# State space's inputs: seven products for six chunks a layer instead of five, their sums of weights on VectorE instead of GpSimd

## The chip, the cores and the metric

The kernel runs on one core of a Trainium2 chip. The metric is the device time of one execution in microseconds; the median of three runs is given, and one more execution was profiled. The core's engines have their own instruction queues and meet only at semaphores: TensorE (PE; its weight loads are listed as PEld), VectorE (DVE), ScalarE (ACT), GpSimd (POOL) and SyncE (SP), which issues the loads of the weights.

## The reference, cut to what matters

Two models of two layers each work on 256 tokens of width 1024, all in float32. The change touches the first model's two layers, in one place: the multiplication of the normed input by the columns of `w_in` that are the inputs of the state space (`xbc`, 3072 columns), the convolution with four taps after it, and silu.

```python
u = rms_norm(h, mix_norm[l])
(z_s, xbc, dt_s, qkv, z_d, b_d, a_d, gate_s, gate_d) = jnp.split(u @ w_in[l], split_points, axis=-1)
...
xbc = jax.nn.silu(causal_depthwise_conv(xbc, conv_w, conv_b))
xs, Bm, Cm = jnp.split(xbc, [SSM_INNER, SSM_INNER + SSM_GROUPS * SSM_STATE], axis=-1)
...
dt = jax.nn.softplus(dt_raw.astype(f32) + dt_bias.astype(f32))
a = -jnp.exp(a_log.astype(f32))
y = ssd_chunked(xs, dt, a, Bm, Cm) + xs.astype(f32) * d_skip.astype(f32)[:, None]
```

## The kernel before, in words

**Chunks.** All weights come from HBM in chunks of 128 x 2048 floats (sixteen tiles of 128 x 128, 1 MB) into a ring of three slots. SyncE loads chunk c once TensorE has begun chunk c-2 (`stream`). Each chunk gives 256 output features for 256 tokens. The twelve chunks of `xbc` are called steps 0 to 11 here; two layers have them, so whatever happens in one layer happens twice.

**Plain or by seven.** A plain chunk is sixteen products of a 128 x 128 weight tile with 256 tokens (`Tensor.product`). A chunk "by seven" (`Tensor.seven`) sees the chunk as a 2 x 2 matrix of blocks and uses Winograd's form of Strassen's method: seven block products in place of eight, each of four tiles with 128 tokens, 28 in all. For it someone must make, beforehand, four sums of weight blocks (the tile `s` in the arena: `s1` to `s4` here, of which `s1` and `s2` come from the first instruction), and, once per stage, four sums of the tokens (`tokens_by_dve`, four instructions, L1103 to L1108). Afterwards VectorE puts the quarters of the result together from two PSUM banks (`join`, L1122 to L1133, four instructions), after ScalarE has copied one quarter out (`part_by_act`, L1017).

**Who waits for the sums.** In the usual order of the seven products TensorE takes B11, B21 and T4 first (24 of 56 records), waits for the first instruction's sums (`summed(2)`), takes T3, waits for the second's (`summed(3)`), takes T2 and T1, and waits for the last (`summed(4)`). In the first chunk of a stage (`new`) the order is another: B11 and B21 (16 records), then at once the wait for all four sums, then B22, T1, T2, T3, T4.

**The steps.** `BY_SEVEN` lists the steps that go by seven, 2, 5, 6, 9 and 10 before. Steps 0 and 1 are multiplied before the norm is known and scaled by VectorE (`pair_opened_by_dve`, L1032). TensorE then multiplies the 48 small columns (`small`, L1999), goes through steps 2 to 11, with transposes of a finished step beside them (`rows`, L2007), and takes the first chunk of the gate z (`z_s` 0). Then it needs the silu of the last step (`features_ready` 12) for the products `cb` (L2039), and VectorE's copy of the first of these (L1703) before it may fill the same bank with `seg` (L2047).

**VectorE's queue.** In this order: norm (L912), scaling of steps 0 and 1, the tokens' sums, the chain that makes the time steps dt from `small` (L1568 to L1601, handing over to ScalarE four times), and then for each step, if it is by seven, the join, and for every step the convolution: six `scalar_tensor_tensor` (L1621), three taps for two tiles, in place. The convolution waits for ScalarE, which first writes the product with the fourth tap and the bias (L1270 for a joined step; L1278 and L1284 for a plain one, which ScalarE reads from PSUM itself). After each step ScalarE makes silu (L1289). After step 11 VectorE waits for a small exponential of ScalarE (`eg1`, L1340), makes the sums of weights for z's first chunk by seven, and copies `cb` (L1703).

**Sums by GpSimd.** For the five steps by seven of each layer the sums of weights are made by GpSimd (`weights_by_pool`, L1086 to L1090). Everywhere else `weights_by_dve` and `last_weights_by_dve` make them on VectorE (L1070, L1072, L1058). A semaphore of each engine counts its sums; `SUMMED` says how many there were before a chunk.

```python
    for n in range(12):
        if n in BY_SEVEN:
            join(v, m.seven_xbc, L, "xbc_7", BY_SEVEN.index(n), in_place=True)
            if ROWS_AT <= n < ROWS_AT + 8:
                rows(n - ROWS_AT)
        conv(n)
```

Of the kernel before, what the change touches and what calls it, by code (L numbers as in the profile page):

```python
# [12 lines left out]
ALU = mybir.AluOpType  # L13
AX = mybir.AxisListType

P = 128
S = 256
# [3 lines left out]
DEPTH = 2  # L21
# [4 lines left out]
RING = 3  # L26
# [115 lines left out]
GROUPS = 4  # L142


class Sems:


    def __init__(self, ctx, nc):
        self.nc, self.all = nc, []

        def sem(name):
            self.all.append(ctx.enter_context(nc.semaphore(name)))
            return self.all[-1]
# [81 lines left out]
        self.angles_ready = sem("angles_ready")  # L235
        self.rotary_ready = sem("rotary_ready")
        self.sum_by_dve = sem("sum_by_dve")
        self.sum_by_pool = sem("sum_by_pool")
        self.tx_by_dve = sem("tx_by_dve")
        self.th_ready = sem("th_ready")  # L240
        self.pool_step = sem("pool_step")
# [10 lines left out]

BY_SEVEN = (2, 5, 6, 9, 10)
Z_SEVEN = (1, 2, 3, 4, 5, 6, 7)
Q_SEVEN = (1, 2, 4, 5, 7, 8, 10, 11)

# [38 lines left out]
class Tensor:  # L297
# [96 lines left out]
    def seven(self, sums, f, at, X, Y, acts, first, last, ready=None, new=False, by_token=False):  # L394


        e, sems = self.e, self.sems
        if at[0] == 0:
            self.whole = self.chunk()
        a = lambda i, g: self.whole[:, (i * GROUPS + g) * P:(i * GROUPS + g + 1) * P]  # L400
        s = lambda i, g: sums.s[:, f % 2, SUM_OF[i], g * P:(g + 1) * P]
        part = lambda bank, i: bank[:, i * P:(i + 1) * P]

        def product(bank, i, weights, what, fresh, stop):
            for g in at:
                if ready:
                    ready(what, g)

                both = (acts(what, g), weights(g)) if by_token else (weights(g), acts(what, g))
                ins = self.mm(part(bank, i), *both, fresh and g == at[0], stop and g == at[-1])  # L410
            return ins

        def summed(n):
            e.wait_ge(sems.sum_by_pool if f in BY_POOL else sems.sum_by_dve, 4 * SUMMED[f] + n)

        def finished(ins):
            if last:
                ins.then_inc(sems.bulk_done, 1)

        product(X, 0, lambda g: a(0, g), "B11", first, False)  # L420
        product(X, 1, lambda g: a(1, g), "B21", False, False)
        if ready:
            summed(4)
            product(Y, 3, lambda g: s(4, g), "B22", first, False)
            if new:
                product(Y, 1, lambda g: s(1, g), "T1", False, False)
            finished(product(X, 2, lambda g: s(2, g), "T2", False, last))
            product(Y, 2, lambda g: s(3, g), "T3", False, False)
            if not new:
                product(Y, 1, lambda g: s(1, g), "T1", False, False)  # L430
            finished(product(Y, 0, lambda g: a(3, g), "T4", False, last))
        else:
            product(Y, 0, lambda g: a(3, g), "T4", first, False)
            summed(2)
            product(Y, 2, lambda g: s(3, g), "T3", False, False)
            summed(3)
            finished(product(X, 2, lambda g: s(2, g), "T2", False, last))
            product(Y, 1, lambda g: s(1, g), "T1", False, False)
            summed(4)
            finished(product(Y, 3, lambda g: s(4, g), "B22", False, last))  # L440
# [237 lines left out]
def loads(c):  # L678

    return c // RING + (c % RING > 0)  # L680
# [36 lines left out]
    multiply_fast(_L, "down", _at + CHUNKS2 - KF // 2, KF // 2, PAIRS, False)  # L717


BY_POOL = {FAST_FROM[_L, "xbc_7"] + _i for _L in range(DEPTH) for _i in range(len(BY_SEVEN))}  # L720
SUMMED = [sum((_g in BY_POOL) == (_f in BY_POOL) for _g in range(_f)) for _f in range(len(FAST))]


def feed(L, name):
# [336 lines left out]
def weights_by_dve(v, seven, ring, f, last=True):  # L1061
# [10 lines left out]
    e.tensor_tensor(s[:, 2, :], s[:, 1, :], w[:, 0, :], ALU.add).then_inc(sems.sum_by_dve, 1)  # L1072
    if last:
        last_weights_by_dve(v, seven, ring, f)


def weights_by_pool(g, seven, ring, f):

    e, sems, c = g.e, g.sems, FAST[f]
    w = ring[:, c % RING, :].rearrange("p (i n) -> p i n", i=4)  # L1080
    s = seven.s[:, f % 2]
    e.wait_ge(sems.w_loaded[c % RING], 16 * loads(c))
    if f >= 2:

        e.wait_ge(sems.w_used, FAST[f - 2] + 1)
    e.tensor_tensor(s[:, 0:2, :], w[:, 2:3, :].to_broadcast([P, 2, GROUPS * P]), w[:, 0:4:3, :], ALU.add).then_inc(sems.sum_by_pool, 2)  # L1086
    e.wait_ge(sems.sum_by_pool, 4 * SUMMED[f] + 2)
    e.tensor_tensor(s[:, 2, :], s[:, 1, :], w[:, 0, :], ALU.add).then_inc(sems.sum_by_pool, 1)
    e.wait_ge(sems.sum_by_pool, 4 * SUMMED[f] + 3)
    e.tensor_tensor(s[:, 3, :], w[:, 1, :], s[:, 2, :], ALU.add).then_inc(sems.sum_by_pool, 1)  # L1090


def tokens_by_dve(v, m, seven, n, at):

    v.e.wait_ge(v.sems.x_ready, scaled(n) + KD)
    sums_by_dve(v, m.xT, seven, at)
# [431 lines left out]
def first_dve(v, m, m2, L, par, par_next, cst, ring, ones):  # L1528
# [33 lines left out]
    for i in range(2):  # L1562
        pair_opened_by_dve(v, m, L, "xbc", i, m.pad[:, i, :, 3:3 + S])
    tokens_by_dve(v, m, m.seven_xbc, 3 * L + 1, TOKENS_FROM[L, "xbc_7"])
    e.wait_ge(sems.chain_done, CHAIN.filled(L, "small", 0))
    b = bk[CHAIN.bank(L, "small", 0)]
    t = lambda i: m.tmp[:, i]
# [98 lines left out]


    for n in range(12):
        if n in BY_SEVEN:
            join(v, m.seven_xbc, L, "xbc_7", BY_SEVEN.index(n), in_place=True)  # L1670
            if ROWS_AT <= n < ROWS_AT + 8:
                rows(n - ROWS_AT)
        conv(n)
        if ROWS_AT <= n < ROWS_AT + 8 and n not in BY_SEVEN:
            rows(n - ROWS_AT)
        if n == CUM_AT:
            running_sums()
        if n == CUM_T_AT:
            e.wait_ge(sems.chain_done, CHAIN.filled(L, "cum_t", 0))
            b = bk[CHAIN.bank(L, "cum_t", 0)]  # L1680
            e.tensor_copy(m.acT[0:3 * SPREAD, :], b[0:3 * SPREAD, 0:S]).then_inc(sems.chain_read_dve, 1)
# [266 lines left out]
def first_pool(g, m, m2, L, cst, ring):  # L1948

    e, sems, seen = g.e, g.sems, g.seen  # L1950
    feed_by_pool(g, m, L, "ffn1")
    for i in range(len(BY_SEVEN)):
        weights_by_pool(g, m.seven_xbc, ring, FAST_FROM[L, "xbc_7"] + i)
    e.wait_ge(sems.chain_done, CHAIN.filled(L, "kq", 3))
    e.memset(m.inv64[0:BASE, :, BASE:2 * BASE], 0.0)
    e.wait_ge(sems.diag_turned, upto(L, "diag_turned", 1))
    e.tensor_copy(m.inv64[0:BASE, :, 0:BASE], m.diag[0:BASE])
    e.tensor_copy(m.inv64[BASE:2 * BASE, :, BASE:2 * BASE], m.diag[BASE:2 * BASE]).then_inc(sems.diag_ready, 1)
    seen.up("diag_ready")
    if L == DEPTH - 1:  # L1960
        e.wait_ge(sems.mem_squared, KD)
        n = KD // 2
        while n:
            ins = e.tensor_tensor(m2.memx[:, 0:n, :], m2.memx[:, 0:n, :], m2.memx[:, n:2 * n, :], ALU.add)
            n //= 2
            if n:
                ins.then_inc(sems.pool_step, 1)
                e.wait_ge(sems.pool_step, seen.up("pool_step"))
            else:
                ins.then_inc(sems.mem_summed, 1)  # L1970
    feed_by_pool(g, m, L, "ffn2")
    seen.check(L)
# [1201 lines left out]
```

## Time and profile before

| | |
|---|---|
| median of three runs | 3200.02 us (3200.02 to 3201.71) |
| the profiled execution | 3200.47 us, of which the span is 3198.7 us |
| TensorE busy | 3180.1 us, 99% of the span; mean granted clock 0.999 |
| VectorE busy | 2349.5 us, 73% |
| ScalarE busy | 663.8 us, 21% |
| GpSimd busy | 278.7 us, 9% |
| weights loaded | 460 whole chunks of 1 MB, median 4.9 us from issue to landing |

The span counts from the first to the last instruction; 1.8 us of the execution lie around it. "Busy" is the time in which an engine had an instruction under way. Matmuls in float32 stand as two records each. Matmul durations overlap their neighbours, so a group's length is best read as the distance from its start to the next group's start. "[0.28 <-DVE arena L1703]" behind a row means that the engine sat idle for 0.28 us before it and that this instruction ended the wait. "x12" is the number of records that a row merges.

### The profile page before, as it was taken

The page shows a single profiled execution, that of the slowest core. Times are in us where ns is not written, and L with a number is a line of the kernel's source. Part 1 is how long each engine was busy: PE and PEld are TensorE (multiplying, and loading weights), DVE is VectorE, ACT ScalarE, POOL GpSimd, SP SyncE. Part 2 cuts the span into 40 slices and gives each one's busy share as a digit, 9 for nine tenths or more (in the row PEclk, how much of TensorE's full clock was granted, in tenths as well). Part 3 has the DMA queues.
Part 4 walks back from the last instruction along what each step waited for, and adds up shares of the span by engine and source line. Part 5 has one row for each costly group of instructions (what it writes and reads, how often), then busy time and mean ns, then how long its engine had stood idle before and what let it go on. Part 6 is the DMA issues. An engine that isn't in the chain of part 4 may idle for free.

```text
span 3198.7 us, 59387 instructions
## 1 busy us (share of the span) xinstructions
PE 3180.1 (99%) x25152; PEld 3032.9 (95%) x25152; DVE 2349.5 (73%) x4622; ACT 663.8 (21%) x1627; POOL 278.7 (9%) x329
## 2 busy tenths in 40 slices
PE   9999999999999999999999999999999999999998
PEld 9999999899999999998999999889999999889998
DVE  6657887376666578873867898877786988876885
ACT  1113433211111134332211111212211111212211
POOL 0202000001102020000011000300031000300031
PEclk9999999999999999999999999999999999999999
DMA  5544444345444443443544454343444444343443
GB/s 204 172 158 137 141 150 154 110 161 172 170 161 170 159 145 133 160 146 112 184 171 172 159 172 170 120 155 138 158 166 165 169 165 169 123 154 132 159 171 132
DMA packets 89786, 497.51 MB, mean 156 GB/s; under 512 B 25104, under 2 KB 29616, under 8 KB 30640
## 3 DMA queue, kind: packets, MB, share of 16 engines
q1 hardware_dynamic: 70752, 489.45, 44.2%
q10 hardware_dynamic: 18768, 4.25, 0.7%
q8 instruction: 199, 3.26, 0.4%
q14 instruction: 67, 0.55, 0.0%
HBM read 491.55 MB, written 2.11 MB: 154 GB/s over the span
## 4 chain that ended last, share of the span: by engine, by line
PE 89%; DVE 8%; ACT 1%; issue 1%; DMA 1%; ACTq 0%; SPq 0%; DVEq 0%
PE bank L358 82%; DVE arena L1070 2%; DVE arena L1058 1%; DVE arena L1072 1%; ACT arena L2430 1%; DVE arena L2702 1%; DVE arena L1125 1%; PE bank L2068 1%; DVE arena L1131 1%; DVE arena L2709 1%; DVE arena L1122 0%; PE bank L2863 0%; PE bank L2122 0%; PE bank L2807 0%; PE bank L2844 0%
## 5 line engine op out<-in xcount | busy, mean ns | idle before, releaser
L358 PE MATMUL bank<-arena 128*128 128x128 f32 x9384 | 1109.9, 275 | 2.2 <-DVE arena L1058 2.2
L358 PEld LDWEIGHTS bank<-arena 128*128 128x128 f32 x9384 | 1078.1, 192 | 2.9 <-DVE arena L1058 2.9
L358 PE MATMUL bank<-arena,ring 128*128 128x128 f32 (+1 forms) x6360 | 994.8, 309 | 2.0 <-ACT arena L876 1.9
L358 PEld LDWEIGHTS bank<-arena,ring 128*128 128x128 f32 x6360 | 900.0, 191 | 58.3 <-issue 2.9
L358 PE MATMUL bank<-xT,ring 128*128 128x128 f32 (+1 forms) x4912 | 693.0, 295 | 0.3 <-DVE arena L1133 0.3
L358 PEld LDWEIGHTS bank<-xT,ring 128*128 128x128 f32 x4912 | 643.5, 192 | 26.7 <-issue 1.0
L1070 DVE TENSOR_TENSOR arena<-ring 128x1024 f32<-128x1024 f32 x349 | 426.2, 1221 | 103.2 <-PE bank L358 99.1
L1017 ACT ACTIVATE arena<-bank 128x128 f32<-128x128 f32 x317 | 87.4, 276 | 1005.3 <-PE bank L358 1000.0
L1125 DVE TENSOR_TENSOR arena<-arena,bank 128x256 f32<-128x256 f32 x317 | 133.6, 422 | 201.4 <-PE bank L358 189.0
L358 PE MATMUL bank<-xT,arena 128*128 128x128 f32 x1976 | 261.9, 275 | 0.7 <-DVE arena L1058 0.6
L1072 DVE TENSOR_TENSOR arena<-arena,ring 128x512 f32<-128x512 f32 x349 | 247.0, 708 | 11.9
L1058 DVE TENSOR_TENSOR arena<-ring,arena 128x512 f32<-128x512 f32 x349 | 246.1, 705 | 11.5
L1122 DVE TENSOR_TENSOR arena<-arena,bank 128x256 f32<-128x256 f32 x317 | 132.3, 417 | 159.4 <-ACT arena L1017 159.4
L358 PEld LDWEIGHTS bank<-xT,arena 128*128 128x128 f32 x1976 | 240.4, 192 | 2.4 <-DVE arena L1058 2.4
L2484 DVE SCALAR_TENSOR_TENSOR arena<-arena,par 128x256 f32<-128x256 f32 x480 | 204.4, 502 | 0.0
L1621 DVE SCALAR_TENSOR_TENSOR arena<-arena,par 128x256 f32<-128x256 f32 x288 | 136.7, 544 | 47.4 <-ACT arena L1284 29.7
L1213 POOL TENSOR_TENSOR arena<-arena 128x128 f32<-128x128 f32 x66 | 54.0, 818 | 1160.7 <-DVE arena L1143 655.1
L1131 DVE TENSOR_TENSOR arena<-bank,arena 128x256 f32<-128x256 f32 x317 | 134.5, 424 | 10.9
L2737 POOL TENSOR_TENSOR arena<-arena 128x512 f32<-128x512 f32 x10 | 44.9, 4494 | 659.9 <-ACT arena L2349 659.7
L1048 ACT ACTIVATE arena<-arena 128x256 f32<-128x256 f32 x88 | 36.8, 418 | 251.3 <-DVE arena L1133 228.9
L1133 DVE TENSOR_TENSOR arena<-arena,bank 128x128 f32<-128x128 f32 x317 | 87.9, 277 | 0.0
L890 ACT ACTIVATE xT<-hT 128x256 f32<-128x256 f32 x96 | 38.6, 412 | 174.5 <-DVE hT L1171 74.9
(329 smaller groups left out, 2126.8 us busy)
## 6 DMA issues: line engine op xcount, KB each, us to landing
ring<-w SPq DMA_DIRECT2D x460, 1024.0 KB, 4.9
hT<-hT_d ACTq DMA_DIRECT2D x4, 256.0 KB, 6.8
ring<-w SPq DMA_DIRECT2D x4, 256.0 KB, 6.6
ring<-w SPq DMA_DIRECT2D x2, 512.0 KB, 4.5
arena<-blocks_d ACTq DMA_DIRECT2D x4, 256.0 KB, 4.7
arena<-base_d ACTq DMA_DIRECT2D x16, 64.0 KB, 4.6
arena<-memT_d SPq DMA_DIRECT2D x1, 1024.0 KB, 8.5
outT<-hT SPq DMA_DIRECT2D x4, 256.0 KB, 2.5
```

What stands on the lines that cost most here:

```text
L358: ins = self.e.matmul(out, lhsT, rhs, start=start, stop=stop)
L1017: e.activation(seven.part[:, i % 2], a.banks[BULK.bank(L, name, (i, 0))][:, 0:P], ACT.Copy).then_inc(sems.part_copied, 1)
L1058: e.tensor_tensor(s[:, 3, :], w[:, 1, :], s[:, 2, :], ALU.add).then_inc(sems.sum_by_dve, 1)
L1070: e.tensor_tensor(s[:, 0:2, :], w[:, 2:3, :].to_broadcast([P, 2, GROUPS * P]), w[:, 0:4:3, :], ALU.add).then_inc(sems.sum_by_dve, 2)
L1072: e.tensor_tensor(s[:, 2, :], s[:, 1, :], w[:, 0, :], ALU.add).then_inc(sems.sum_by_dve, 1)
L1122: e.tensor_tensor(quarter[:, 0:2, 0, :], twice(a), X[:, 1:3, :], ALU.add).then_inc(sems.bulk_read_dve, 1)
L1125: e.tensor_tensor(quarter[:, 0:2, 1, :], twice(u), Y[:, 1:3, :], ALU.subtract).then_inc(sems.dve_step, 1)
L1131: e.tensor_tensor(last, Y[:, 0:2, :], twice(w), ALU.subtract).then_inc(sems.dve_step, 1)
L1133: e.tensor_tensor(quarter[:, 0, 1, :], quarter[:, 0, 1, :], Y[:, 3, :], ALU.add).then_inc(sems.bulk_read_dve, 1)
L1213: e.tensor_tensor(th[0], low[:, P:S], low[:, 0:P], ALU.subtract).then_inc(sems.pool_step, 1)
L1621: ins = stt(y, m.pad[:, n % 2, kk, tap:tap + S], col(w, 4 * tile + tap), y, ALU.mult, ALU.add)
L2484: ins = stt(y, x, w, y, ALU.mult, ALU.add)
```

## The change

Four things. The steps by seven become 2, 4, 6, 8, 10 and 11: six a layer in place of five, so step 5 and step 9 become plain, and steps 4, 8 and 11 go by seven. All sums of weights of these steps are made by VectorE, and GpSimd's function and semaphore go. In VectorE's queue the sums of step 2 stand behind the tokens' sums, ahead of the time steps' chain; those of every other step n stand at the beginning of step n-1, ahead of that step's join and convolution. And `join` now writes into the padded tile of the step's own parity, given by `to=`, since the number of a step among those by seven no longer has the step's parity.

```diff
-BY_SEVEN = (2, 5, 6, 9, 10)
+BY_SEVEN = (2, 4, 6, 8, 10, 11)
...
         def summed(n):
-            e.wait_ge(sems.sum_by_pool if f in BY_POOL else sems.sum_by_dve, 4 * SUMMED[f] + n)
+            e.wait_ge(sems.sum_by_dve, 4 * SUMMED[f] + n)
...
-BY_POOL = {FAST_FROM[_L, "xbc_7"] + _i for _L in range(DEPTH) for _i in range(len(BY_SEVEN))}
-SUMMED = [sum((_g in BY_POOL) == (_f in BY_POOL) for _g in range(_f)) for _f in range(len(FAST))]
+SUMMED = list(range(len(FAST)))
...
     tokens_by_dve(v, m, m.seven_xbc, 3 * L + 1, TOKENS_FROM[L, "xbc_7"])
+    weights_by_dve(v, m.seven_xbc, ring, FAST_FROM[L, "xbc_7"])
     e.wait_ge(sems.chain_done, CHAIN.filled(L, "small", 0))
...
     for n in range(12):
+        if n + 1 in BY_SEVEN and n > 1:
+            weights_by_dve(v, m.seven_xbc, ring, FAST_FROM[L, "xbc_7"] + BY_SEVEN.index(n + 1))
         if n in BY_SEVEN:
-            join(v, m.seven_xbc, L, "xbc_7", BY_SEVEN.index(n), in_place=True)
+            join(v, m.seven_xbc, L, "xbc_7", BY_SEVEN.index(n), in_place=True, to=m.pad[:, n % 2, :, 3:3 + S])
...
     feed_by_pool(g, m, L, "ffn1")
-    for i in range(len(BY_SEVEN)):
-        weights_by_pool(g, m.seven_xbc, ring, FAST_FROM[L, "xbc_7"] + i)
```

**How the queues read.** Rows of a queue give line, operation, operands and shape; line numbers of the changed kernel are those of its own file, some 2 lower near the helpers and 17 or 18 lower further down. First, VectorE from the tokens' sums (L1103 to L1108; L1085 to L1090 in the changed kernel) into the chain of the time steps (L1568, L1551). Before:

```order
L1103 TENSOR_TENSOR arena<-xT 128x512
L1105 TENSOR_TENSOR arena<-arena,xT 128x512
L1107 TENSOR_TENSOR arena<-xT 128x512
L1108 TENSOR_TENSOR arena<-xT,arena 128x512
L1568 TENSOR_TENSOR arena<-bank,par 128x96
L1572 SCALAR_TENSOR_TENSOR arena<-arena 128x96
```

Of the changed kernel, the same place:

```order
L1089 TENSOR_TENSOR arena<-xT 128x512
L1090 TENSOR_TENSOR arena<-xT,arena 128x512
L1068 TENSOR_TENSOR arena<-ring 128x1024
L1070 TENSOR_TENSOR arena<-arena,ring 128x512
L1056 TENSOR_TENSOR arena<-ring,arena 128x512
L1551 TENSOR_TENSOR arena<-bank,par 128x96
```

The three instructions that make step 2's sums (L1068, L1070, L1056) now stand between the tokens' sums and the time steps' chain.

Second, VectorE from the convolutions of steps 0 and 1 (the row x12) over the join of step 2 to the convolution of step 3. Before:

```order
L1621 SCALAR_TENSOR_TENSOR arena<-arena,par 128x256 x12
L1122 TENSOR_TENSOR arena<-arena,bank 128x2x128
L1125 TENSOR_TENSOR arena<-arena,bank 128x2x128
L1131 TENSOR_TENSOR arena<-bank,arena 128x256
L1133 TENSOR_TENSOR arena<-arena,bank 128x128
L1621 SCALAR_TENSOR_TENSOR arena<-arena,par 128x256 x12
L1632 TENSOR_TENSOR arena<-bank,small 128x256 x2
```

Of the changed kernel (L1104 to L1115 is the join, L1604 the convolution):

```order
L1604 SCALAR_TENSOR_TENSOR arena<-arena,par 128x256 x12
L1104 TENSOR_TENSOR arena<-arena,bank 128x2x128
L1107 TENSOR_TENSOR arena<-arena,bank 128x2x128
L1113 TENSOR_TENSOR arena<-bank,arena 128x256
L1115 TENSOR_TENSOR arena<-arena,bank 128x128
L1604 SCALAR_TENSOR_TENSOR arena<-arena,par 128x256 x6
L1068 TENSOR_TENSOR arena<-ring 128x1024
L1070 TENSOR_TENSOR arena<-arena,ring 128x512
L1056 TENSOR_TENSOR arena<-ring,arena 128x512
L1604 SCALAR_TENSOR_TENSOR arena<-arena,par 128x256 x6
L1615 TENSOR_TENSOR arena<-bank,small 128x256 x2
```

The sums of step 4 stand between the convolutions of step 2 and step 3.

Third, TensorE from step 3 to the transposes behind step 4; a plain step is the row with 128x256. Before:

```order
L358 MATMUL bank<-xT,ring 128x256 x16
L2007 MATMUL bank<-cst,arena 128x128 x4
L358 MATMUL bank<-xT,ring 128x256 x16
L2007 MATMUL bank<-cst,arena 128x128 x4
L358 MATMUL bank<-xT,ring 128x128 x8
```

Of the changed kernel:

```order
L357 MATMUL bank<-xT,ring 128x256 x16
L1990 MATMUL bank<-cst,arena 128x128 x4
L357 MATMUL bank<-xT,ring 128x128 x8
L357 MATMUL bank<-arena,ring 128x128 x4
L357 MATMUL bank<-arena 128x128 x12
L357 MATMUL bank<-xT,arena 128x128 x4
L1990 MATMUL bank<-cst,arena 128x128 x4
```

Step 4 was plain and goes by seven: B11 and B21 (x8), T4 (x4), then the three products whose weights are sums (x12), and the last (x4).

## Rows read from the trace of the kernel before

**Rows 1.** The page, part 1: busy us, share of the span, instructions.

```profile
PE 3180.1 (99%) x25152; PEld 3032.9 (95%) x25152; DVE 2349.5 (73%) x4622; ACT 663.8 (21%) x1627; POOL 278.7 (9%) x329
```

**Rows 2.** The waits of TensorE: us in total, times, longest us.

```profile
PE bank L358 <- DVE arena L1058: 2.7, 5, 0.6
PE bank L1985 <- DVE ones L1537: 1.9, 1, 1.9
```

**Rows 3.** Stretches, both layers: length, busy PE, PEld, DVE, ACT, POOL, granted clock, DMA.

```profile
235.10:312.50 77.40, 77.40 (x517) 72.30 (x517) 56.39 (x135) 26.58 (x53) 20.13 (x12) 1.00 0.44 150
1113.30:1190.70 77.40, 77.40 (x517) 72.30 (x517) 56.37 (x134) 26.57 (x53) 20.01 (x12) 1.00 0.44 150
```

**Rows 4.** Timeline of TensorE, first layer, steps 2 to 5: start us, us.

```profile
235.14 2.02 PE L358 MATMUL bank<-xT,ring 128*128 128x128 f32 x16
...
241.46 7.07 PE L358 MATMUL bank<-xT,ring 128*128 128x256 f32 x32
248.37 0.60 PE L2007 MATMUL bank<-cst,arena 128*128 128x128 f32 x4
248.81 7.07 PE L358 MATMUL bank<-xT,ring 128*128 128x256 f32 x32
...
256.15 1.95 PE L358 MATMUL bank<-xT,ring 128*128 128x128 f32 x16
...
258.83 2.84 PE L358 MATMUL bank<-arena 128*128 128x128 f32 x24
...
262.41 0.60 PE L2007 MATMUL bank<-cst,arena 128*128 128x128 f32 x4
```

**Rows 5.** Timeline of VectorE, first layer, tokens' sums to step 3.

```profile
234.50 0.68 DVE L1108 TENSOR_TENSOR arena<-xT,arena 128x512 f32<-128x512 f32 x1
235.34 0.26 DVE L1568 TENSOR_TENSOR arena<-bank,par 128x96 f32<-128x96 f32 x1 [0.16 <-PE bank L1999]
...
241.53 4.84 DVE L1621 SCALAR_TENSOR_TENSOR arena<-arena,par 128x256 f32<-128x256 f32 x12 [2.23 <-ACT arena L1270]
246.28 0.41 DVE L1122 TENSOR_TENSOR arena<-arena,bank 128x256 f32<-128x256 f32 x1
...
249.04 11.20 DVE L1621 SCALAR_TENSOR_TENSOR arena<-arena,par 128x256 f32<-128x256 f32 x12 [1.16 <-ACT arena L1270]
```

**Rows 6.** Timeline of VectorE, sums for z's first chunk by seven.

```profile
312.53 1.22 DVE L1070 TENSOR_TENSOR arena<-ring 128x1024 f32<-128x1024 f32 x1
313.79 0.69 DVE L1072 TENSOR_TENSOR arena<-arena,ring 128x512 f32<-128x512 f32 x1
314.51 0.69 DVE L1058 TENSOR_TENSOR arena<-ring,arena 128x512 f32<-128x512 f32 x1
315.12 1.94 DVE L1703 TENSOR_TENSOR arena<-bank,cst 128x384 f32<-128x384 f32 x4
```

**Rows 7.** Timeline, all engines, a wait of TensorE for such sums.

```profile
24.48 0.69 DVE L1058 TENSOR_TENSOR arena<-ring,arena 128x512 f32<-128x512 f32 x1
...
25.22 0.97 PEld L358 LDWEIGHTS bank<-xT,arena 128*128 128x128 f32 x8 [0.75 <-DVE arena L1058]
```

**Rows 8.** Timeline of GpSimd, first layer, step 5's sums.

```profile
247.08 2.36 POOL L1086 TENSOR_TENSOR arena<-ring 128x1024 f32<-128x1024 f32 x1 [18.99 <-issue]
...
250.94 1.33 POOL L1090 TENSOR_TENSOR arena<-ring,arena 128x512 f32<-128x512 f32 x1
```

**Rows 9.** Timelines of TensorE, VectorE and ScalarE, first layer, end of the stage.

```profile
298.94 13.98 PE L358 MATMUL bank<-xT,ring 128*128 128x256 f32 x64
...
315.82 1.23 PE L2047 MATMUL bank<-small 120*128 120x256 bf16 x6 [0.28 <-DVE arena L1703]
...
300.95 2.46 DVE L1621 SCALAR_TENSOR_TENSOR arena<-arena,par 128x256 f32<-128x256 f32 x6 [0.50 <-ACT arena L1270]
307.60 2.46 DVE L1621 SCALAR_TENSOR_TENSOR arena<-arena,par 128x256 f32<-128x256 f32 x6 [4.18 <-ACT arena L1284]
...
310.09 0.63 ACT L1289 ACTIVATE arena<-arena 128x512 f32<-128x512 f32 x1 [2.01 <-DVE arena L1621]
```

More of the change, by code:

```diff
@@ L237, in __init__ @@
         self.sum_by_dve = sem("sum_by_dve")
-        self.sum_by_pool = sem("sum_by_pool")
         self.tx_by_dve = sem("tx_by_dve")
@@ L1074, in weights_by_dve @@
         last_weights_by_dve(v, seven, ring, f)
[L1077 to L1090, printed above, removed]
 def tokens_by_dve(v, m, seven, n, at):
```

## The prediction

> **What bounds the kernel now.** First the page's busy times: TensorE has work under way for 99% of the span, VectorE for 73%, GpSimd for 9% [rows 1]. Then the waits of TensorE: the longest single one is 1.9 us at the very start, and all its waits for sums of weights come to 2.7 us [rows 2]. Then the stretches: from the first record of step 2 to the end of z's first chunk TensorE is busy 77.40 of 77.40 us in both layers, at the full granted clock (1.00, the 2.4 GHz level), VectorE 56.4 [rows 3]. So the time is TensorE's work in its own order, and an edit counts in two ways only: by the records it takes off TensorE, and by the waits that it makes there. The two layers' stretches are alike to 0.02 us in every column but GpSimd's [rows 3]; I work out the first and double it.
>
> **TensorE's records.** A plain step takes 248.37 - 241.46 = 6.91 us, one by seven 262.41 - 256.15 = 6.26 [rows 4]. Steps 4, 8 and 11 change to seven and steps 5 and 9 back: one more net, 0.65 us less per layer. That is all that this change can give, 1.3 us in all.
>
> **The price of a set of sums on VectorE.** The three instructions start at 312.53, 313.79 and 314.51 and the next independent one at 315.12 [rows 6]: the queue is held for 2.59 us (1.26 + 0.72 + 0.61); the first result is there 1.22 us after the start, the last after 2.67. GpSimd needed 250.94 + 1.33 - 247.08 = 5.19 [rows 8]. TensorE's weight load starts 0.05 us after the sum's end (24.48 + 0.69 = 25.17, then 25.22) [rows 7]; I add 0.1 us for the load ahead of its matmul, which no row gives singly (between 0 and 0.12, its share of that row of eight in 0.97 us).
>
> **Step 2.** VectorE's last tokens' sum starts at 234.50 [rows 5], the next instruction can start 0.61 later, as behind L1058, so at 235.11. Step 2's sums then are whole at 235.11 + 2.67 = 237.78. TensorE begins step 2 at 235.14 and in this order wants all four after 16 records; 24 records take 258.83 - 256.15 = 2.68 us [rows 4], so 16 take 1.79: it is there at 236.93. It waits until 237.78 + 0.05 + 0.1 = 237.93, **1.0 us**. Before, GpSimd had made them while TensorE was still busy with the steps 0 and 1. Nothing covers this wait.
>
> **What queues behind.** The time steps' chain starts not at 235.34 [rows 5] but at 235.11 + 2.59 = 237.70: 2.36 us late. ScalarE and VectorE hand that chain to and fro without a gap that TensorE sets, so the convolutions of steps 0 and 1 start 2.36 us late as well (241.53 before), and so do the join of step 2 (246.28) and the convolution of step 2 (249.04) [rows 5].
>
> **Step 4.** Its sums stand behind that convolution. Six of its kind take (246.28 - 241.53) / 2 = 2.38 us when nothing disturbs them; the row from 249.04 has twelve in 11.20 us in place of 4.75, beside GpSimd's sums from 247.08 on [rows 5, 8]. With GpSimd gone I take 2.38. So VectorE reaches step 4's sums at 249.04 + 2.38 + 2.36 = 253.78, the first is there at 255.00, and TensorE goes on at 255.15. TensorE began step 4 at 248.81 [rows 4], now 1.0 later, and after 24 records, at 248.81 + 1.0 + 2.68 = 252.49, it wants this sum. It waits **2.66 us**. The later sums of step 4 come in time (0.89 us of records stand between each two waits, 0.72 between the sums). The transfer of step 4's weights plays no part: it is issued when step 2 begins, at 235.14, and step 5's, issued at 241.46, lay in the ring at 247.08 [rows 4, 8].
>
> If the convolution kept its disturbed pace, this wait would be 5.6 - 2.4 = 3.2 us longer; that is the upper end, taken for no part of the forecast since no other work is on GpSimd then.
>
> **Steps 5 to 11.** I carry the same queue on by the same durations, with ScalarE's part (part copy, join, two activations, convolution). VectorE gets six sets of sums and one join of about 1.6 us more in this stretch, 17 us, and gets back at least 11.20 - 4.75 = 6.45. 56.4 + 17 - 6.4 = 67 of about 80 us: it isn't the bound by its sum. By the order the first sums of steps 6, 8, 10 and 11 lie ready 3.8 to 4.6 us before TensorE wants them. Step 11 is the last that could go wrong: its join can start 0.5 us ahead of the bank's being full. So TensorE loses nothing here, and at the end of step 11 it is 1.0 + 2.66 - 0.65 = 3.01 us late.
>
> **The end of the stage.** Step 11 was plain and goes by seven. Before, step 10 (by seven) ended at 298.94 - 0.44 = 298.50, 0.44 being the transposes (248.81 - 248.37), and its convolution started at 300.95, 2.45 later; step 11 (plain) ended at 298.94 + 6.91 = 305.85, its convolution started at 307.60, 1.75 later [rows 4, 9]. A joined step's way is 0.70 us longer. Behind it hangs a chain without slack: silu (2.49 us on), VectorE's sums for z (2.44 on), the copy of cb (2.59 on), TensorE's seg, which already waits 0.28 us for it at 315.82 [rows 6, 9]. Now 308.86 + 2.45 + 2.49 + 2.44 + 2.59 + 0.70 = 319.53, which is **3.71 us** after 315.82. The last term, 0.70, is copy to seg (315.82 - 315.12).
>
> **The sum.** Per layer +1.0 + 2.66 + 0.70 - 0.65 = +3.71; twice, +7.4 us. After seg both engines stand to each other as before, so nothing is handed back: TensorE has no idle time there to absorb it. The profiled execution took 3200.47 us (span 3198.7 and 1.8 around it): 3207.9. The median of the runs is 3200.02, 0.45 below it; I say **3207.7 us**, 0.23% more. A measurement of this kernel can tell about 0.2%, 6.4 us, from no change, so the forecast lies just outside.
>
> GpSimd's disturbance of VectorE also goes from the norm and steps 7 and 8. The Trainium skill, SBUF — State Buffer, "Who interferes with whom", says that VectorE and GpSimd lock a shared port pair against each other, one of them standing still. By that rule the disturbed row is explained and its removal is a gain; the trace agrees in the row (11.20 for 4.75), but the sum is not changed by it, since TensorE never waited for those convolutions.
>
> **The rivals.**
>
> *VectorE comes in time (13%).* If step 4's sums began by 251.05, 2.7 us earlier than I find, and step 2's by 234.2, the waits would not be, and only the end's 0.70 and the 0.65 would stand: 3200.5 us; with the wait of step 2 alone 3202.5. For it speaks that VectorE idles 21 us of this stretch [rows 3] and loses GpSimd's disturbance, 6.45 us in one row. Against it: the disturbed row begins at 249.04, and everything I count up to there was undisturbed; the idle time lies later. The Trainium skill's GPSIMD Engine Reference, "Engine selection", is for this rival: elementwise work of two inputs belongs on VectorE, GpSimd being some 2 times slower. The trace agrees on the ratio (5.19 to 2.67), but a slower engine that begins early is early still.
>
> *VectorE falls behind at the end (8%).* Its margin at step 11 is 0.5 us. If each joined step costs 0.5 us more than I count (the copies of the running sums fall in step 5, beside a set of sums), the joins of steps 10 and 11 and with them silu and seg come 1 to 2 us later per layer: 3210 to 3212.
>
> *The clock falls (4%).* TensorE stands still for 2.7 us in a place where it never did. The rows show 1.00 in both stretches [rows 3], and the wait of 1.9 us at the start stands ahead of any work. If the granted clock fell to 1.2 GHz for the length of one plain step behind each long wait, that step would take twice 6.91: +6.9 per layer, 3221.5 us. The Trainium skill, TensorE: Matmul & The Clock Gate, "What's actually happening", says that an idle TensorE falls back to half its clock; no run here has shown that yet.
>
> **How the numbers follow.** The forecast has 75%, of which some 14 lie below 3206.4, since 1.3 us of margin is as much as the terms of 0.1 to 0.5 us may be off, twice. Same is that 14, 11 of the first rival: 25%. Faster is the 2 left of it. Slower is 61 + 8 + 4 = 73%. Range: 3203.8 (both waits a third shorter) to 3211.5 (the second rival), leaving out most of the first rival and the clock.
>
> **What would show it.** In the waits of TensorE, VectorE's L1056 (the last of three sums) twice with about 1 us and its L1068 (the first) twice with about 2.7; the wait of seg at about 1.0 in place of 0.28. GpSimd without 20 us in each stretch. The convolutions of steps 2 and 3 at 2.4 us each. From step 2's start to seg 84.4 us in place of 80.7, in both layers, and no other change anywhere. It is wrong if step 4 starts its third product at once, if the stretches from z on are not as long as before, or if the granted clock leaves 1.00.

## The result, and the profile after

The changed kernel took 3211.88 us in the median of six runs (3209.48 to 3212.48), the kernel before 3200.59 in the same comparison: ratio 1.0033, 95% interval 1.0023 to 1.0042. That is slower, by 11.3 us, where the forecast was 7.7 more than the kernel before (3207.7 against 3200.02; 7.4 by the sum). The median lies 0.4 us above the upper end of the range; counted from the kernel before it is 11.3 against 11.5, just inside it. In two later comparisons the same kernel took 3209.26 (1.0025, 1.0016 to 1.0034) and 3209.06 (1.0024, 1.0014 to 1.0033), 7.8 and 7.7 us more than before. One run of the kernel before in the second comparison took 7310.18 us; it enters no ratio, and nothing here explains it. The profiled execution took 3212.48 us, its span 3210.7.

The waits of TensorE in the changed kernel, first four rows; L357 is every large matmul, L1068 the first and L1056 the last instruction of a set of sums:

```profile
PE bank L357 <- DVE arena L1068: 4.9, 2, 2.4
PE bank L357 <- DVE arena L1056: 3.5, 6, 0.7
PE bank L357 <- ACT arena L874: 2.6, 1, 2.6
PE bank L2030 <- DVE arena L1688: 1.9, 2, 1.0
```

Against [rows 2], the first row is new (two waits of 2.4 us, one per layer), the second has two of 0.7 more, at step 2 (and one less, near 25 us, in a part that the change does not touch), and the last is seg's, 0.97 twice, 0.28 before [rows 9]. Those are the three places of the prediction. The third row is the start of the program, of which below.

TensorE's timeline of the second layer, steps 2 to 4 and the end:

```profile
1122.01 2.02 PE L357 MATMUL bank<-xT,ring 128*128 128x128 f32 x16
1124.69 1.16 PE L357 MATMUL bank<-xT,arena 128*128 128x128 f32 x8 [0.67 <-DVE arena L1056]
...
1129.26 7.07 PE L357 MATMUL bank<-xT,ring 128*128 128x256 f32 x32
...
1136.61 1.95 PE L357 MATMUL bank<-xT,ring 128*128 128x128 f32 x16
...
1141.90 2.94 PE L357 MATMUL bank<-arena 128*128 128x128 f32 x24 [2.45 <-DVE arena L1068]
...
1145.57 0.60 PE L1990 MATMUL bank<-cst,arena 128*128 128x128 f32 x4
...
1206.37 1.23 PE L2030 MATMUL bank<-small 120*128 120x256 bf16 x6 [0.97 <-DVE arena L1688]
```

Step 2 takes 1129.26 - 1122.01 = 7.25 us where it took 6.32 [rows 4]: +0.93. (The idle time in the row is only 0.67: without a gap the records on both sides would have overlapped by 0.16, and the eight behind it took 0.11 more.) Step 4 by seven takes 1145.57 - 1136.61 = 8.96, of which 6.26 are its records: +2.70. From step 2 to seg it is 1206.37 - 1122.01 = **84.36 us; 80.67 before**, that is +3.69.

VectorE's timeline of the first layer, where the sums now stand:

```profile
228.07 0.67 DVE L1030 TENSOR_TENSOR arena<-bank,rstd 128x512 f32<-128x512 f32 x1
...
233.83 0.69 DVE L1030 TENSOR_TENSOR arena<-bank,rstd 128x512 f32<-128x512 f32 x1 [5.09 <-PE bank L357]
...
237.09 1.22 DVE L1068 TENSOR_TENSOR arena<-ring 128x1024 f32<-128x1024 f32 x1
...
239.68 0.25 DVE L1551 TENSOR_TENSOR arena<-bank,par 128x96 f32<-128x96 f32 x1
...
253.36 2.46 DVE L1604 SCALAR_TENSOR_TENSOR arena<-arena,par 128x256 f32<-128x256 f32 x6 [1.16 <-ACT arena L1252]
255.74 1.22 DVE L1068 TENSOR_TENSOR arena<-ring 128x1024 f32<-128x1024 f32 x1
```

The sums for step 2 hold the queue for 239.68 - 237.09 = 2.59 us, and the convolution of step 2 (L1604) takes 255.74 - 253.36 = 2.38, undisturbed: it was one half of a row of 11.20 us [rows 5]. VectorE idles 5.09 us ahead of scaling step 1, in front of the sums that come too late. Most of that gap is new with the change. Before, it was 0.87 us: the eight instructions of the norm ran beside GpSimd's sums for step 2 and took 7.47 us where they now take 3.26. The kernel before, then the changed kernel:

```profile
222.89 7.47 DVE L912 SCALAR_TENSOR_TENSOR xT<-hT,par,rstd 128x256 f32<-128x256 f32 x8 [2.32 <-ACT rstd L899]
224.87 3.26 DVE L910 SCALAR_TENSOR_TENSOR xT<-hT,par,rstd 128x256 f32<-128x256 f32 x8 [2.32 <-ACT rstd L897]
```

TensorE's timeline of the first layer and the stretches around step 4's third product; columns as in [rows 3]:

```profile
257.01 4.35 PE L357 MATMUL bank<-arena 128*128 128x128 f32 x24 [2.44 <-DVE arena L1068]
261.20 1.06 PE L357 MATMUL bank<-xT,arena 128*128 128x128 f32 x8
```

```profile
252.00:256.00 4.00, 2.57 (x23) 2.38 (x22) 2.84 (x9) 3.15 (x7) 0.00 (x0) 1.00 0.68 236
256.00:257.00 1.00, 0.00 (x0) 0.00 (x0) 0.97 (x2) 0.48 (x1) 0.00 (x0) 0.78 0.26 107
257.00:258.00 1.00, 0.99 (x4) 0.99 (x5) 0.97 (x2) 0.00 (x0) 0.00 (x0) 0.50 0.00 0
...
260.00:261.00 1.00, 1.00 (x11) 1.00 (x11) 1.00 (x3) 0.28 (x1) 0.00 (x0) 1.00 0.00 0
```

Here the 24 records after the wait took 261.20 - 257.01 = 4.19 us; in the second layer 2.78. The granted clock stood at 0.50, the 1.2 GHz level, until 260. This stretch (237.13 to 322.88) is 85.75 us, **+5.07**. The 12.0 us by which the span is longer are: the start +1.99 (step 2 begins at 237.13, not 235.14), the first stretch +5.07, what lies between the two stretches +1.61, the second stretch +3.69, the rest -0.36.

The start is no part of the change, and it holds something that stays open. TensorE waited there for ScalarE (the third row of its waits), and the first 32 matmuls of 128x256 took 18.19 - 8.24 = 9.95 us, where 32 such records take 6.91 in a plain step:

```profile
8.24 10.11 PE L357 MATMUL bank<-arena,ring 128*128 128x256 f32 x32 [2.56 <-ACT arena L874]
18.19 0.59 PE L530 MATMUL bank<-xT,ones 128*128 128x256 f32 x2
```

From 10 to 12 us six of them ran, and eleven in the kernel before. The granted clock stands at 1.00 in both (the columns are the length, TensorE's busy time and records, the clock, and DMA):

```profile
10.00:12.00 2.00, 2.00 (x6) 1.00 0.31 27
10.00:12.00 2.00, 2.00 (x11) 1.00 0.12 41
```

"Step 4's sums early as well" and "other steps" below show the same slow records at a clock of 1.00 (32 in 9.05 and 9.03 us), and three other kernels show them with the clock at 0.50. So here the granted clock of the rows does not tell all, and no run shows what else it was.

### The profile page after: what moved, and what is told of

Its sections match the earlier page's. It is cut to its first block, busy times and chain, and to the rows that moved or that the text cites. A ratio compares the mean times of both kernels' runs of the same rounds, so it can differ in the third digit from the quotient of the medians.

```text
span 3210.7 us, 59501 instructions
## 1 busy us (share of the span) xinstructions
PE 3184.9 (99%) x25200; PEld 3038.5 (95%) x25200; DVE 2355.0 (73%) x4666; ACT 663.1 (21%) x1627; POOL 228.1 (7%) x299
## 3 DMA queue, kind: packets, MB, share of 16 engines
q8 instruction: 199, 3.26, 0.4%
## 4 chain that ended last, share of the span: by engine, by line
PE 88%; DVE 9%; ACT 2%; issue 1%; DMA 0%; DVEq 0%; ACTq 0%
PE bank L357 82%; DVE arena L1068 2%; DVE arena L1056 1%; DVE arena L1070 1%; ACT arena L2413 1%; DVE arena L2685 1%; DVE arena L1107 1%; DVE arena L1113 1%; DVE arena L1604 1%; PE bank L2051 1%; DVE arena L2692 1%; DVE arena L1104 0%; PE bank L2846 0%; PE bank L2105 0%; PE bank L2790 0%
## 5 line engine op out<-in xcount | busy, mean ns | idle before, releaser
L357 PE MATMUL bank<-arena 128*128 128x128 f32 x9432 | 1117.2, 275 | 7.0 <-DVE arena L1068 4.9
L357 PEld LDWEIGHTS bank<-arena 128*128 128x128 f32 x9432 | 1085.1, 192 | 8.2 <-DVE arena L1068 5.3
L357 PE MATMUL bank<-arena,ring 128*128 128x128 f32 (+1 forms) x6376 | 1000.7, 310 | 2.6 <-ACT arena L874 2.6
L357 PEld LDWEIGHTS bank<-arena,ring 128*128 128x128 f32 x6376 | 905.1, 192 | 59.4 <-issue 2.9
L357 PE MATMUL bank<-xT,ring 128*128 128x128 f32 (+1 forms) x4880 | 683.0, 294 | 0.1
L357 PEld LDWEIGHTS bank<-xT,ring 128*128 128x128 f32 x4880 | 635.1, 192 | 24.5 <-issue 0.7
L1068 DVE TENSOR_TENSOR arena<-ring 128x1024 f32<-128x1024 f32 x361 | 442.6, 1226 | 101.5 <-PE bank L357 101.0
L357 PE MATMUL bank<-xT,arena 128*128 128x128 f32 x1992 | 264.1, 276 | 1.4 <-DVE arena L1056 1.3
L1070 DVE TENSOR_TENSOR arena<-arena,ring 128x512 f32<-128x512 f32 x361 | 254.2, 704 | 12.3
L1056 DVE TENSOR_TENSOR arena<-ring,arena 128x512 f32<-128x512 f32 x361 | 253.9, 703 | 11.9
L1104 DVE TENSOR_TENSOR arena<-arena,bank 128x256 f32<-128x256 f32 x319 | 133.1, 417 | 159.8 <-ACT arena L1015 159.6
L357 PEld LDWEIGHTS bank<-xT,arena 128*128 128x128 f32 x1992 | 242.4, 192 | 3.3 <-DVE arena L1056 3.3
L2467 DVE SCALAR_TENSOR_TENSOR arena<-arena,par 128x256 f32<-128x256 f32 x480 | 204.3, 497 | 0.0
L1604 DVE SCALAR_TENSOR_TENSOR arena<-arena,par 128x256 f32<-128x256 f32 x288 | 118.1, 479 | 38.1 <-ACT arena L1252 18.9
L1115 DVE TENSOR_TENSOR arena<-arena,bank 128x128 f32<-128x128 f32 x319 | 88.4, 277 | 0.0
```

Of the source, the lines that this page charges most:

```text
L357: ins = self.e.matmul(out, lhsT, rhs, start=start, stop=stop)
L1104: e.tensor_tensor(quarter[:, 0:2, 0, :], twice(a), X[:, 1:3, :], ALU.add).then_inc(sems.bulk_read_dve, 1)
L1115: e.tensor_tensor(quarter[:, 0, 1, :], quarter[:, 0, 1, :], Y[:, 3, :], ALU.add).then_inc(sems.bulk_read_dve, 1)
L1604: ins = stt(y, m.pad[:, n % 2, kk, tap:tap + S], col(w, 4 * tile + tap), y, ALU.mult, ALU.add)
L2467: ins = stt(y, x, w, y, ALU.mult, ALU.add)
```

## The experiments

Each was timed in turns with the kernel before, of which three comparisons gave medians of 3201.50, 3201.36 and 3201.39 us. "Stretch" is from step 2's first record to seg.

**The changed kernel again** (no edit).

> The changed kernel once more, for the parts that aren't settled by one profile. Theory (waits by place, plus the clock): the stretch from step 2's start to seg is 84.4 us wherever the granted clock stays at 1.00, and 85.8 where it falls behind step 4's wait of 2.4 us; the start of the program, which the change does not touch, is some us shorter or longer from run to run. Time 3208 to 3212.5, depending on how many of these falls one execution has. Rival (the whole 11 us are waits of this stage): both stretches at 85.8 or more, in every run, and the time within 0.5 us of 3211.9.

Measured: 3209.26 us (ten runs, 3206.84 to 3211.89). Stretches 85.98 and 84.35 us. The first layer's clock fell behind step 4's wait again (mean from 240 to 280 us: 0.96). In the second it had fallen already as step 2 began, right behind the small columns (the first row):

```profile
1115.08 3.67 PE L1982 MATMUL bank<-par,xT 128*128 128x48 f32 x32
1118.58 3.65 PE L357 MATMUL bank<-xT,ring 128*128 128x128 f32 x16
1122.03 1.09 PE L357 MATMUL bank<-xT,arena 128*128 128x128 f32 x8
...
1138.46 2.94 PE L357 MATMUL bank<-arena 128*128 128x128 f32 x24 [1.74 <-DVE arena L1068]
```

Step 2's first 16 records took 3.45 us in place of 1.86, and the wait for step 2's sums was gone, that at step 4 was 1.74 in place of 2.45, and the stretch as long as ever. A slow TensorE ahead of a wait costs nothing: VectorE's time sets the end of the wait. The rival falls, since one stretch was 84.35.

**Step 2's sums early** (sums ahead of the scaling of step 1).

```diff
     for i in range(2):
+        if i == 1:
+            weights_by_dve(v, m.seven_xbc, ring, FAST_FROM[L, "xbc_7"])
         pair_opened_by_dve(v, m, L, "xbc", i, m.pad[:, i, :, 3:3 + S])
     tokens_by_dve(v, m, m.seven_xbc, 3 * L + 1, TOKENS_FROM[L, "xbc_7"])
-    weights_by_dve(v, m.seven_xbc, ring, FAST_FROM[L, "xbc_7"])
```

> The changed kernel with step 2's sums moved ahead of the scaling of step 1, where VectorE idles 5.1 us. Theory: no wait at step 2, the time steps' chain back at its old place, so step 4's sums 2.4 us earlier; TensorE still waits 1.2 us at step 4 and 1.0 at seg. Stretch 81.8 us in both layers, no fall of the clock, time 3200.6 + 2.3 = 3202.9. Rival (VectorE has too much work in this stretch, wherever it stands): the waits move to later steps, stretch 83 or more, time above 3206.

Measured: 3203.31 us, ratio 1.0008 (0.9999 to 1.0017), stretches 82.02 and 82.01, TensorE's waits in the first of them:

```profile
253.08 2.94 PE L357 MATMUL bank<-arena 128*128 128x128 f32 x24 [1.04 <-DVE arena L1068]
317.55 1.23 PE L2031 MATMUL bank<-small 120*128 120x256 bf16 x6 [0.97 <-DVE arena L1689]
```

One set of sums moved in VectorE's own queue to 8.5 us ahead of step 2's start, where it had begun with it: the same work on the same engine. That gave back 2.3 us a layer, and the clock fell at neither step 4 in this profile. The same six sets of sums are made, so VectorE's load is not the cause.

**Step 4's sums early as well.**

```diff
     for n in range(12):
-        if n + 1 in BY_SEVEN and n > 1:
+        if n == 1:
+            weights_by_dve(v, m.seven_xbc, ring, FAST_FROM[L, "xbc_7"] + 1)
+        if n + 1 in BY_SEVEN and n > 3:
             weights_by_dve(v, m.seven_xbc, ring, FAST_FROM[L, "xbc_7"] + BY_SEVEN.index(n + 1))
```

> As early2, and step 4's sums between the convolutions of steps 0 and 1. Theory: no wait for sums at all; the join of step 2 is 2.6 us later and TensorE waits 0.4 to 0.6 us for its bank at step 4's start, and 1.0 at seg. Stretch 81.2 us, time 3200.6 + 1.0 = 3201.6. Rival (VectorE's load): as for early2, above 3205.

Measured: 3202.61 us, ratio 1.0004 (0.9995 to 1.0013), stretches 81.35 and 81.36. The wait at step 4 is now for the bank that step 2's join has to free, and it is 0.41 us, one in each layer:

```profile
249.42 2.02 PE L357 MATMUL bank<-xT,ring 128*128 128x128 f32 x16 [0.41 <-DVE arena L1104]
```

**Six by seven, sums left to GpSimd** (the kernel before; only `BY_SEVEN` and `to=` changed).

```diff
-BY_SEVEN = (2, 5, 6, 9, 10)
+BY_SEVEN = (2, 4, 6, 8, 10, 11)
...
-            join(v, m.seven_xbc, L, "xbc_7", BY_SEVEN.index(n), in_place=True)
+            join(v, m.seven_xbc, L, "xbc_7", BY_SEVEN.index(n), in_place=True, to=m.pad[:, n % 2, :, 3:3 + S])
```

> The kernel before with only the steps changed to 2, 4, 6, 8, 10, 11 and the joins into the padded tile; the sums stay with GpSimd. Theory: GpSimd makes step 4's sums from 240.7 to 246, in time for TensorE, but beside the convolutions of steps 0 and 1, which it holds up by 3.6 us, so the join of step 2 frees the bank for step 4 1.5 us late; seg waits 1.0. Stretch 80.7 + 1.5 = 82.2 us, time 3200.6 + 3.0 = 3203.6. Rival (the sums' engine is all that matters): no wait at step 4, time 3200.6 + 0.1. Rival (the choice of steps costs it all, not the engine): stretch above 84, time above 3207.

Measured: 3204.38 us, ratio 1.0010 (1.0001 to 1.0019), stretches 82.05 and 82.34 (in the second the clock had fallen by itself within step 2's first records). GpSimd, VectorE and TensorE around step 4:

```profile
240.76 2.35 POOL L1086 TENSOR_TENSOR arena<-ring 128x1024 f32<-128x1024 f32 x1 [12.24 <-issue]
241.65 8.13 DVE L1621 SCALAR_TENSOR_TENSOR arena<-arena,par 128x256 f32<-128x256 f32 x12 [2.23 <-ACT arena L1270]
...
249.70 0.41 DVE L1122 TENSOR_TENSOR arena<-arena,bank 128x256 f32<-128x256 f32 x1
250.21 2.02 PE L358 MATMUL bank<-xT,ring 128*128 128x128 f32 x16 [1.11 <-DVE arena L1122]
```

The convolutions of steps 0 and 1 take 8.13 us beside GpSimd's sums, 4.84 alone [rows 5], and the join is late by that. So with GpSimd's sums TensorE waits at step 4 too, by another way: 1.1 us in place of 2.4. With these steps no place of the sums that was tried makes the stretch as short as before: 81.35 at best, in "step 4's sums early as well", against 80.67.

**Step 4's sums later still** (behind the convolution of step 3).

```diff
-        if n + 1 in BY_SEVEN and n > 1:
+        if n + 1 in BY_SEVEN and n > 3:
...
         conv(n)
+        if n == 3:
+            weights_by_dve(v, m.seven_xbc, ring, FAST_FROM[L, "xbc_7"] + 1)
```

> The changed kernel with step 4's sums one convolution later still, behind that of step 3: the wait at step 4 grows from 2.4 to 4.8 us. Theory of the clock (a long wait lets it fall, for about 3 us, and that costs 1.5): it now falls in both layers in every execution; stretch 84.4 + 2.4 + 1.5 = 88.3 us in both, time 3200.6 + 15 = 3216. Rival (the fall in the first layer comes from something else there, and the wait plays no part): the second layer's stretch is 86.8 at a clock of 1.00, time 3212 to 3214.

Measured: 3217.22 us (3216.45 to 3217.55), ratio 1.0049 (1.0036 to 1.0061), stretches 88.36 and 89.28. TensorE behind the wait in the second layer:

```profile
1143.02 5.49 PE L357 MATMUL bank<-arena 128*128 128x128 f32 x24 [4.82 <-DVE arena L1068]
1148.31 1.10 PE L357 MATMUL bank<-xT,arena 128*128 128x128 f32 x8
```

Behind a wait of 4.8 us the clock fell in both layers; 24 records took 5.29 us here and 4.41 (first layer) in place of 2.78. The first layer is as forecast. In the second the clock was down for some 7 us and not 3, from within the wait on, and the stretch is 1 us over the forecast:

```profile
1140.00:1142.00 2.00, 0.00 (x0) 0.00 (x0) 2.00 (x6) 0.12 (x1) 0.00 (x0) 0.89 0.01 4
1142.00:1144.00 2.00, 0.98 (x4) 0.98 (x5) 1.93 (x3) 0.00 (x0) 0.00 (x0) 0.50 0.00 0
...
1146.00:1148.00 2.00, 2.00 (x11) 2.00 (x11) 0.42 (x1) 0.28 (x1) 0.00 (x0) 0.50 0.00 0
```

**Other steps** (six by seven, sums as in the change, steps 2, 5, 6, 8, 9, 10).

```diff
-BY_SEVEN = (2, 4, 6, 8, 10, 11)
+BY_SEVEN = (2, 5, 6, 8, 9, 10)
```

> The changed kernel with the steps 2, 5, 6, 8, 9 and 10 by seven: six a layer, sums by VectorE in the same way, but step 4 plain and step 11 plain. Theory: VectorE has step 5's sums ready before they are wanted; left are the wait of 0.8 at step 2 and the 0.3 at seg. Stretch 81.0 us in both layers, no fall of the clock behind a wait, time 3200.6 + 0.6 = 3201.2. Rival (six sets of sums are too much for VectorE): waits at other steps, stretch above 83, time above 3205.

Measured: 3200.57 us, ratio 0.9999 (0.9990 to 1.0008), stretches 80.94 and 81.64 (in the second the clock had fallen at 1114 us, within step 2's first records). One line of numbers takes 8 to 9 us off the changed kernel. Six sets of sums by VectorE cost nothing but the wait of 0.67 us at step 2 (0.93 us of the step).

**Seven steps, sums in VectorE's idle time.** Built on "step 2's sums early".

```diff
-BY_SEVEN = (2, 4, 6, 8, 10, 11)
+BY_SEVEN = (2, 5, 6, 7, 9, 10, 11)
...
+    weights_by_dve(v, m.seven_z, ring, FAST_FROM[L, "z_7"])
     e.wait_ge(sems.small_by_act, upto(L, "small_by_act", 5))
...
-    weights_by_dve(v, m.seven_z, ring, FAST_FROM[L, "z_7"])
     for g in range(SSM_GROUPS):
```

> A version that should beat both: seven steps by seven (2, 5, 6, 7, 9, 10, 11), step 2's sums ahead of the scaling of step 1, and the sums for z's first chunk ahead of VectorE's wait for eg1. Theory: no wait of TensorE in the stretch; 2 x 0.65 off and the 0.28 at seg gone: stretch 79.1 us, time 3200.6 - 3.2 = 3197.4, 0.1% less. Rival (VectorE's load): seven sets and two more joins need more than there is, waits appear at step 7 or 11, stretch 80.5 or more, time 3200 or above.

Measured: **3196.13 us** (eleven runs, 3195.47 to 3200.90), ratio 0.9985 (0.9976 to 0.9994), faster than both kernels. Of the 5.2 us between the medians 3.5 are the two stretches; the rest lies outside them, in the profiled executions 0.9 us at the start, which no edit touches, and 0.4 us in each layer's seg. Stretches 78.92 in both layers, in which TensorE waits for nothing:

```profile
234.28:311.00 76.72, 76.72 (x568) 73.23 (x568) 66.58 (x162) 25.81 (x51) 0.00 (x0) 1.00 0.44 151
```

VectorE is busy for 66.6 of 76.7 us, 87%, without being late anywhere in the stretch.

**Seven steps, z's sums late** (the last edit undone).

> As seven_steps, but the sums for z's first chunk stay behind VectorE's wait for eg1, as in both kernels. Theory: the chain silu, eg1, sums, copy of cb, seg is what the end waits for, and with steps 9, 10 and 11 all by seven VectorE reaches it late: TensorE waits 1.5 us at seg in place of none, stretch 78.9 + 1.5 = 80.4 us, time 3196.1 + 3.0 = 3199.1. Rival (the sums' place at the end does not matter, the step count gave all of seven_steps' gain): stretch 78.9 to 79.2, time 3196 to 3197.

Measured: 3201.21 us, ratio 0.9998 (0.9990 to 1.0007), stretches 80.53 and 80.54, 1.6 us more each, with the wait at seg:

```profile
315.37 1.23 PE L2031 MATMUL bank<-small 120*128 120x256 bf16 x6 [1.45 <-DVE arena L1689]
```

Of the 1.75 us by which the fastest kernel's stretch is shorter than before, the place of one set of sums at the end decides over 1.6. (The median is 2 us over the forecast; its profiled execution took 3199.81.)

**The kernel before again** (no edit).

> The kernel before once more, for its spread and its clock. Theory: both stretches 80.7 us at 1.00; where the execution is longer than 3200.5 it is so by the start, by a fall of the clock near 560 to 600 us or near 1080 to 1120 us, at 1.5 us each, which has nothing to do with the change. Rival (such falls come with the change): none of them in this profile, and all runs within 0.5 us.

Measured: 3200.43 us (3199.51 to 3203.57), ratio 0.9999; stretches 80.67 twice. Its profile shows no fall before the program's end, so neither side of the expectation was met in full: the runs spread over 4 us, not 0.5, and where in this kernel the clock falls was not seen. That it plays a part is in the mean granted clock of each execution: in the three comparisons 16 runs of the kernel before have 0.998 and took 3202.11 to 3203.91 us, 62 have 0.999 and took at most 3202.42. In other kernels falls were seen where no edit changes what TensorE does: before 12 us (step 2's sums early, step 4's sums later, seven steps with z's late), between 581 and 591 us (the changed kernel, both early), between 1114 and 1122 us (the changed kernel again, other steps, six by GpSimd).

**The changed kernel a third time** (no edit).

> The changed kernel a third time, for the fall of the clock behind step 4's wait: seen in the first layer in both profiles so far, and in the second in neither. Theory (a wait of 2.4 us is near the edge, and it depends on where it falls in time): a stretch is 84.4 us without a fall and 85.7 to 86.0 with one, nothing between or beyond; time 3208 to 3212. Rival (the fall belongs to the first layer): 85.8 in the first and 84.4 in the second again. Both allow the same picture once more; only a fall in the second layer or none in the first tells them apart.

Measured: 3209.06 us (3207.49 to 3210.20). Stretches 84.35 and 85.97, the other way round:

```profile
255.38 2.94 PE L357 MATMUL bank<-arena 128*128 128x128 f32 x24 [2.44 <-DVE arena L1068]
...
1137.25 4.58 PE L357 MATMUL bank<-arena 128*128 128x128 f32 x24 [2.44 <-DVE arena L1068]
```

The same wait of 2.44 us, once with and once without a fall. So the fall is no matter of the layer. Over three profiles three of the five waits of 2.44 or 2.45 us had it; the sixth wait, of 1.74 us with a fall some 16 us before it, had none. The fall came at 256.6 us within the wait (the changed kernel), at 255.1 as TensorE resumed (again), and here at 1138.3, when TensorE had been at work for 1 us.

## Why the prediction was right, and where its size was off

By its own steps:

- **TensorE's records** (-0.65 a layer): right. Step by step, plain and by seven took 6.91 and 6.26 us again.
- **Step 2** (+1.0): measured +0.93, of which the row of the wait shows 0.67. "Step 2's sums early" took the wait away and put the time steps' chain back.
- **What queues behind** (2.36 us late) and **step 4** (+2.66): measured 2.33 us late and +2.70. Moving step 2's sums alone brought the wait from 2.44 to 1.04. The convolution did run at 2.38 us with GpSimd gone, as taken.
- **Steps 5 to 11** (nothing): right, no wait of TensorE there in the profiles of the changed kernel. In the first, the first sums of steps 6, 8, 10 and 11 lay ready 3.8 to 5.5 us ahead (3.8 to 4.6 forecast), and VectorE was busy for 63.3 us up to the end of z's first chunk (67 forecast).
- **The end** (+0.70): the wait at seg went from 0.28 to 0.97. That the chain behind silu has no slack is what the pair of kernels with seven steps shows.
- **The sum per layer**, +3.71: 3.69 in the stretch without a fall of the clock, three times in three profiles (84.36, 84.35, 84.35).

What was off is the clock. The prediction priced it as a rival at +6.9 a layer with 4%, for the length of a plain step, and held the forecast free of it; by its own sign ("if the granted clock leaves 1.00") it was wrong there. The place was right and both numbers were wrong: the clock fell behind three of five waits of 2.4 us, and cost 1.4 to 1.6 us each time (85.75, 85.98, 85.97 against 84.35), since it was down for some 3 us and only the part behind the wait counts. That is 1.5 us on average for the two layers, and up to 3 in one execution. The sentence from the Trainium skill, TensorE: Matmul & The Clock Gate, "What's actually happening", that an idle TensorE falls back to half its clock, is now borne out by this kernel where TensorE idled: 0.50 in the rows above, and in both layers behind 4.8 us.

Of the 11.3 us of the first comparison, 7.4 are the sum and up to 3 such falls behind step 4's waits. In its profiled execution 3.6 more were no part of the stage: 2.0 at the start and 1.6 between 586 and 594 us, where the clock fell (0.50 from 588 to 591) in a part the change does not touch. The other two comparisons, at 7.8 and 7.7, agree with sum and clock together (8.9) to 1.2 us. The first one's runs had more of the low clock: a mean of 0.998 in four of six, and these are the longest (3211.74 to 3212.48; the other two 3209.48 and 3210.54). It was 0.998 in six of ten in the second comparison and in one of ten in the third. Whether that is chance or has a reason is open; only one execution of each set is profiled.

The rivals: "VectorE comes in time" needed step 4's sums 2.7 us earlier; they came at the time that the forecast gave, to within 0.1 us. "VectorE falls behind at the end" did not happen at six steps; with seven, and z's sums left in their place, it did in small: the wait at seg was 1.45 us and not 0.97. The range's upper end, 3211.5, came from that rival, which was not what made the kernel slower. That 11.3 us still lie within the range is luck: the forecast with a fall in both layers would be about 3211.

Three figures of the prediction do not follow from its own sum. The median before and the sum give 3200.02 + 7.4 = 3207.4, not 3207.7. "Both waits a third shorter" takes 2.4 us off and gives 3205.3; the lower end, 3203.8, needs waits shorter by half. And the convolution at its disturbed pace, called the upper end, would be 6.4 us more for two layers, which lies outside the range that is stated.

## What to carry to other kernels

When the bound engine never waits, an edit that moves work to another engine is priced by the moment at which each product lies ready against the moment at which it is wanted, and by everything that queues behind the moved work; the busy share is no guide (VectorE's was 73% of the stretch in the kernel before and 87% in the fastest). Look for the idle gaps of that engine first: here two gaps, of 5.1 us ahead of scaling step 1 (most of it opened by taking the sums off GpSimd) and 2.3 us ahead of eg1, could take the sums for nothing, and using them, with seven steps chosen so that step 4 is plain, turned +0.25% into -0.15%. The choice of steps counts as much: with step 4 plain, the late sums for step 5 cost nothing. And write the timetable in absolute time of the late engine: whatever happens to the waiting one ahead of the wait is free.

## What the hardware showed that was not expected

TensorE's clock fell to 0.50 behind an idle time of only 2.4 us, in three of five cases, and for about 3 us, most of it while matmuls ran again back to back: a wait's cost was 2.7 or 4.2 us with nothing in the program to tell which. There were falls behind shorter idle times as well: at the start of three executions (step 2's sums early, step 4's sums later, seven steps with z's late) the clock fell for about 3 us, some 1 us behind waits of 1.98, 1.87 and 1.90. In the other nine that first wait was 1.47 to 1.68 us, or 2.56 in the changed kernel, and their rows show no fall there; that the waits made the falls is not shown for this place. Behind 4.8 us it fell both times, once for about 3 us and once for about 7.

It also fell where TensorE was never idle: for about 3 us behind the 32 matmuls of 48 columns (1114 to 1117 us in "other steps"; in two more of the twelve profiles, and in the second layer only) and among the small matmuls (588 to 591 us in the changed kernel). A fall ahead of a wait was absorbed whole (84.35 us with it and without).
